# The first RMS norm and the two parts of h at the start of a two-block transformer kernel: squares along rows, multiplied rows turned

## The chip, the core and the metric

The kernel is one program on one core of a Trainium2 chip. Its time is the device time of one execution in microseconds (us). The kernel before takes 2472.72 us, the median of 3 runs (2471.85 to 2472.84).

## The reference, cut to what matters

The reference runs two blocks over one sequence of 512 tokens of width 1024. All numbers are float32. The change concerns the first lines of the first block:

```python
ada = (c @ w_ada[l] + b_ada[l])[:, None, :]
sh1, sc1, gt1, sh2, sc2, gt2 = jnp.split(ada, 6, axis=-1)
h = rms_norm(x, norm1_w[l]) * (1.0 + sc1) + sh1      # x * rsqrt(mean(x*x) + 1e-6) * norm1_w
proj = h @ w_in[l]                                   # 1024 x (4608 + 3360 + 2048)
...                                                  # attention over three dilations, RWKV-7 over 16 heads, gates
x = x + gt1 * ((g_att * y_att + g_rwkv * y_rwkv) @ w_o[l])
...                                                  # conv FFN, then the second block with two layers and their FFNs
```

In the code of the kernel `mod` holds `ada` by columns (partition = feature within a tile of 128, one column for each tile), and `gain1` is `(1 + sc1) * norm1_w`. So tile k of h is `x / rms * gain1[k] + mod[k]`.

## The kernel before

Activations lie with features on the partitions: x and h are 8 tiles (k = 0 to 7) of 128 features by 512 tokens. x arrives by rows (128 tokens on the partitions, 4 groups of 1024 features, tile `x_rows`), and TensorE turns it by multiplying with an identity (`turn`, L312).

Every product of a weight with h is done in three: the weight and h are each split in a high part (rounded to fp32r) and a low part (the rest). TensorE adds w_high x h_high, w_high x h_low and w_low x h_high in a PSUM bank. For a block of weights ("unit", 128 columns) ScalarE makes w_high (`round_unit`, L298) and GpSimd w_low (`lower_unit`, L305). SyncE's queue loads the weights in the order of a ring of four slots; a slot's next load waits for w_low of what was in it.

The order on each engine is written out by hand. The beginning (`begin_pe`, `begin_act`, `begin_dve`) does this:

- SyncE loads x, then 8 blocks of w_ada of 1 MB each (`ada_w`), then four units of w_in. ScalarE's queue loads the first vectors.
- TensorE turns the 32 blocks of x; VectorE and ScalarE copy the 8 turned tiles out of PSUM in turn. ScalarE squares each tile (`sq`), VectorE adds the squares in `rinv`. One product with a matrix of ones sums over the features and spreads the sum to all partitions. VectorE and ScalarE make the root (`rinv`, 128 x 512), and VectorE multiplies the 8 tiles by it into the room of `x_rows` (L548).
- TensorE multiplies c by the blocks of w_ada (`ada_rows_pe`), which gives four lines of 512. VectorE and ScalarE copy two lines each out of PSUM (L447). TensorE makes columns of them (`ada_columns_pe`), VectorE adds the bias and makes `mod` and `gain1` (L453, L458).
- For each tile, ScalarE makes h_high out of the multiplied tile (L525), VectorE makes the shifted tile in float32 (`sq`, L555) and subtracts h_high for h_low (L565). TensorE multiplies the first two units' w_high with both parts as tiles come, and then both w_low with h_high. After that the steady work of the attention stage begins.

`keep_x` stores x to memory for later; it stands in SyncE's queue behind loads of the ring.

Of the kernel before, what the change touches and what calls it, by code (L numbers as in the profile page):

```python
# [15 lines left out]
P = 128  # L16
S = 512
# [103 lines left out]
class Kernel:  # L121
# [327 lines left out]
    def ada_columns_dve(self):  # L449
        V, S_ = self.V, self.S  # L450
        for i in self.ADA_LINES:
# [3 lines left out]
            if i >= 2:  # L455
                at = 4 * (i - 2)
                V.wait_ge(*self.own("dve"))
                V.scalar_tensor_tensor(self.gain1[:, at:at + 4], self.mod[:, 4 * i:4 * i + 4], 1.0,  # L458
                                       self.cols("norm1_w", 4, at), ALU.add, ALU.mult).then_inc(*S_.dve_ada("gain", i))

    def begin_pe(self):
# [7 lines left out]
        for f in range(DT):  # L469
# [5 lines left out]
            self.emptied[b] = (S_.dve_setup if f % 2 else S_.act_setup, ("x", f))  # L475
# [25 lines left out]

    def begin_act(self):
        A, S_ = self.A, self.S
        A.wait_ge(*S_.pool_setup.at("rows"))
        self.load_vectors(0, A, S_.first_loaded)
        for f in range(DT):
            if f % 2 == 0:
                A.wait_ge(*S_.turned.at("x", f))
                A.copy(self.x[:, f, :], self.bank[2 + f % 4][:]).then_inc(*S_.act_setup("x", f))
                A.wait_ge(*self.own("act"))  # L510
            else:
                A.wait_ge(*S_.dve_setup.at("x", f))
            if f >= 2:
                A.wait_ge(*S_.dve_norm.at("norm1", "added", f - 2))
            A.activation(self.sq[:, f % 2, :], self.x[:, f, :], ACT.Square).then_inc(*S_.act_norm("norm1", "square", f))
        A.activation(self.spare[:], self.ones[:, 0:1], ACT.Ln).then_inc(*S_.act_norm())
        self.root_act("norm1")
# [10 lines left out]
    def rooted(self, k):  # L528

        return self.xrow[:].rearrange("p t d -> p (t d)")[:, k * S:(k + 1) * S]  # L530

    def begin_dve(self):
        V, S_ = self.V, self.S
        V.memset(self.rinv[:], 0.0).then_inc(*S_.dve_norm())
        V.wait_ge(*S_.turned.at("vec", 0))
        V.tensor_copy(self.vec[:, 0:P], self.bank[1][:, 0:P]).then_inc(*S_.dve_setup("vec", 0))
        for f in range(DT):
            if f % 2:
# [2271 lines left out]
```

## Time and profile before

| | |
|---|---|
| median of 3 runs | 2472.72 us |
| the profiled execution | 2470.49 us |
| its span, from first to last instruction | 2469.3 us |
| TensorE matmuls busy | 2337.9 us, 95% |
| TensorE weight loads busy | 1847.0 us, 75% |
| VectorE busy | 1433.1 us, 58% |
| ScalarE busy | 686.1 us, 28% |
| GpSimd busy | 882.9 us, 36% |
| mean granted TensorE clock | 0.975 of 2.4 GHz |

The profile is of one execution. Its rows are read as "start, duration, engine, line, operation, output <- inputs, count", and in square brackets the engine's idle time before it and what ended it. A float32 product with a moving operand of 512 columns shows as two records if its weights are float32 and as one if they are fp32r. Records of TensorE overlap their neighbours: what one costs is the distance from start to start. The granted clock is in parts of 2.4 GHz: 0.50 is 1.2 GHz.

### The profile page before, as it was taken

The page shows a single profiled execution, that of the slowest core. Times are in us where ns is not written, and L with a number is a line of the kernel's source. Part 1 is how long each engine was busy: PE and PEld are TensorE (multiplying, and loading weights), DVE is VectorE, ACT ScalarE, POOL GpSimd, SP SyncE. Part 2 cuts the span into 40 slices and gives each one's busy share as a digit, 9 for nine tenths or more (in the row PEclk, how much of TensorE's full clock was granted, in tenths as well). Part 3 has the DMA queues.
Part 4 walks back from the last instruction along what each step waited for, and adds up shares of the span by engine and source line. Part 5 has one row for each costly group of instructions (what it writes and reads, how often), then busy time and mean ns, then how long its engine had stood idle before and what let it go on. Part 6 is the DMA issues. An engine that isn't in the chain of part 4 may idle for free.

```text
span 2469.3 us, 33874 instructions
## 1 busy us (share of the span) xinstructions
PE 2337.9 (95%) x14384; PEld 1847.0 (75%) x14384; DVE 1433.1 (58%) x1805; ACT 686.1 (28%) x854; POOL 882.9 (36%) x415
## 2 busy tenths in 40 slices
PE   6999998999998799899999988999999999999998
PEld 4776775666665688678888866888888887888887
DVE  4221324577667411766675568888863457888733
ACT  3222113434442423222222221322222332322212
POOL 4322221111110344344444433444444444444443
PEclk8999999999999899989999989999999999999999
DMA  6433332212110333223333323233333322333331
GB/s 235 128 103 111 111 103 68 51 41 51 43 45 14 107 98 94 86 77 94 98 112 94 90 62 88 86 102 95 95 110 95 93 86 85 98 98 94 113 94 58
DMA packets 412038, 222.56 MB, mean 90 GB/s; under 512 B 33823, under 2 KB 409458, under 8 KB 410610
## 3 DMA queue, kind: packets, MB, share of 16 engines
q1 hardware_dynamic: 387234, 208.23, 29.2%
q10 hardware_dynamic: 24656, 12.18, 1.8%
q8 instruction: 114, 1.87, 0.3%
q14 instruction: 34, 0.28, 0.0%
HBM read 214.61 MB, written 5.77 MB: 89 GB/s over the span
## 4 chain that ended last, share of the span: by engine, by line
PE 59%; DVE 6%; issue 1%; ACT 1%; POOL 0%; DVEq 0%; ACTq 0%
PE bank L309 59%; DVE ev_s L2406 0%; DVE h_low L2014 0%; DVE mg_r_low L1992 0%; DVE g_c L2216 0%; PE bank L312 0%; DVE ev_low L2418 0%; DVE x_res L2363 0%; DVE sq L653 0%; DVE sq L649 0%; DVE ev_z L2373 0%; DVE ev_c L2375 0%; DVE ev_c L2382 0%; DVE ev_s L2409 0%; DVE sq L2113 0%
## 5 line engine op out<-in xcount | busy, mean ns | idle before, releaser
L305 POOL TENSOR_TENSOR w_low<-w_raw,w_high 128x1024 fp32r<-128x1024 f32 (+1 forms) x331 | 849.5, 2568 | 1494.7 <-ACT w_high L298 1494.6
L309 PE MATMUL bank<-h_high,w_high 128*128 128x512 f32 x2008 | 809.0, 403 | 28.4 <-DVE h_low L660 9.6
L309 PE MATMUL bank<-h_low,w_high 128*128 128x512 f32 x2008 | 789.3, 393 | 0.0
L298 ACT CAST w_high<-w_raw 128x1024 fp32r<-128x1024 f32 (+1 forms) x331 | 358.5, 1084 | 913.2 <-PE bank L309 899.6
L309 PE MATMUL bank<-h_high,w_low 128*128 128x512 f32 x2008 | 510.5, 394 | 0.0
L309 PEld LDWEIGHTS bank<-h_high,w_high 128*128 128x128 f32 x2008 | 379.9, 189 | 133.7 <-issue 24.8
L309 PEld LDWEIGHTS bank<-h_high,w_low 128*128 128x128 f32 x2008 | 377.0, 189 | 84.2 <-issue 4.6
L309 PEld LDWEIGHTS bank<-h_low,w_high 128*128 128x128 f32 x2008 | 381.3, 190 | 78.1 <-issue 3.4
L309 PE MATMUL bank<-g_high,w_high 128*128 128x512 f32 x352 | 138.1, 392 | 2.3 <-ACT g_c L2195 2.3
L309 PE MATMUL bank<-g_low,w_high 128*128 128x512 f32 x352 | 137.8, 391 | 0.0
L2092 DVE TENSOR_TENSOR x_res<-bank,x_res 128x512 f32<-128x512 f32 x32 | 22.1, 692 | 164.8 <-PE bank L309 164.8
L2214 DVE SCALAR_TENSOR_TENSOR g_c<-g_c,vec 128x511 f32<-128x511 f32 x44 | 110.2, 2504 | 1.5
L2225 DVE CAST g_high<-g_c 128x512 fp32r<-128x512 f32 x44 | 102.1, 2320 | 1.5
L2115 DVE TENSOR_TENSOR rinv<-rinv,sq 128x512 f32<-128x512 f32 x48 | 97.5, 2031 | 1.6
L309 PE MATMUL bank<-g_high,w_low 128*128 128x512 f32 x352 | 85.9, 392 | 0.0
L827 DVE COPY att_coming<-bank 128x512 f32<-128x512 f32 x24 | 16.6, 692 | 118.7 <-PE bank L309 118.7
L2240 DVE TENSOR_SCALAR f_c<-bank,vec 128x512 f32<-128x512 f32 x44 | 35.6, 810 | 75.1 <-PE bank L309 72.5
L309 PEld LDWEIGHTS bank<-g_high,w_high 128*128 128x128 f32 x352 | 66.2, 188 | 17.4 <-ACT g_c L2195 3.2
L2195 ACT ACTIVATE g_c<-g_c,vec 128x512 f32<-128x512 f32 x44 | 31.9, 724 | 165.1 <-DVE g_c L2216 165.1
L309 PEld LDWEIGHTS bank<-g_low,w_high 128*128 128x128 f32 x352 | 66.2, 188 | 14.4
L309 PEld LDWEIGHTS bank<-g_high,w_low 128*128 128x128 f32 x352 | 66.2, 188 | 14.4
L1999 DVE TENSOR_TENSOR att_masks<-att_masks,bank 128x512 f32<-128x512 f32 x16 | 10.9, 686 | 109.5 <-PE bank L309 109.5
(375 smaller groups left out, 2886.2 us busy)
## 6 DMA issues: line engine op xcount, KB each, us to landing
w_raw<-in_w_in SPq DMA_DIRECT2D x58, 512.0 KB, 4.7
w_raw<-in_w_up SPq DMA_DIRECT2D x44, 512.0 KB, 3.8
w_raw<-in_w_ffn_gate SPq DMA_DIRECT2D x44, 512.0 KB, 3.8
w_raw<-in_w_ffn_up SPq DMA_DIRECT2D x44, 512.0 KB, 3.8
w_raw<-in_w_ffn_down SPq DMA_DIRECT2D x32, 704.0 KB, 4.5
w_raw<-in_w_ada SPq DMA_DIRECT2D x32, 512.0 KB, 3.6
w_raw<-in_w_down SPq DMA_DIRECT2D x16, 704.0 KB, 4.5
w_raw<-in_w_in ACTq DMA_DIRECT2D x21, 512.0 KB, 4.1
```

The costliest lines, as they stand in the source:

```text
L298: self.A.copy(self.w_high[:, u % SPLIT_SLOTS, 0:k * P], self.raw_of(key)[:, 0:k * P]).then_inc(*self.S.rounded(*key))
L305: self.G.tensor_tensor(self.w_low[:, slot, 0:k * P], self.raw_of(key)[:, 0:k * P], self.w_high[:, slot, 0:k * P].bitcast(F32), ALU.subtrac ...
L309: return self.T.matmul(out, lhsT, rhs, start=start, stop=stop, skip_group_check=True)
L827: return copy(out, in_order(self.bank[b][:], g))
L1999: V.tensor_tensor(self.gate[:, j, :], self.gate[:, j, :], self.bank[4 * (n % 2) + 2 + j][:], ALU.mult).then_inc(*S_.dve_merge())
L2092: V.tensor_tensor(x, bank, x, ALU.add).then_inc(*S_.residual(name, n))
L2115: V.tensor_tensor(total[:], total[:], square, ALU.add).then_inc(*self.S.dve_norm(*key))
L2195: A.activation(gate, gate, ACT.Silu, bias=biases(0)[:, n:n + 1]).then_inc(*S_.silu(name, n))
L2214: V.scalar_tensor_tensor(gate[:, 1:S], scaled[:, 0:S - 1], tap[1], gate[:, 1:S], ALU.mult, ALU.add).then_inc(*S_.parts())
L2225: V.tensor_copy(self.f_high[:, n, :], gate).then_inc(*S_.parts())
L2240: V.tensor_scalar(out, bank[:], tap[2], biases(j)[:, n:n + 1], ALU.mult, ALU.add).then_inc(*S_.parts())
```

## The change

The sum of squares is made along the rows of x as they arrive: ScalarE squares each of the four groups (128 x 1024) and gives the sum of each row (`accum_out`) in `x_root`, 128 x 4. The root is made of these 4 columns. VectorE multiplies the rows in place by it, and copies all 8 turned tiles of x. The multiplied rows are then turned by TensorE a second time (`rooted_pe`), the first before the columns, two more behind them and the others in front of the products of tile k - 3. ScalarE makes h_high directly from PSUM. For even tiles VectorE makes the whole tile (`begin_whole`, from PSUM) and subtracts h_high; for odd tiles ScalarE takes the shift off h_high again (`less`, with `shift_less` = -mod), and VectorE makes h_low with one operation from PSUM. `keep_x` waits for the copies of x.

The diff, without `ada_columns_dve` (it makes `shift_less` behind `mod` for the two shift lines) and the allocations:

```diff
 def begin_pe(self):
...
         for k in range(DT):
-            if k == 3:
-                self.sum_pe("norm1", S_.dve_norm.at("norm1", "squares"))
-                self.emptied[7] = (S_.dve_norm, ("norm1", "mean"))
             self.ada_rows_pe(k)
+        self.emptied[1] = (S_.act_norm, ("row", self.ADA_LINES[-1]))
+        T.wait_ge(*S_.dve_norm.at("norm1", "rooted", 3))
+        self.rooted_pe(0)
         self.ada_columns_pe()
         self.end("pe", "ada")
+        self.rooted_pe(1)
+        self.rooted_pe(2)
...
         for k in range(DT):
+            if k + 3 < DT:
+                self.rooted_pe(k + 3)
             T.wait_ge(*S_.h_low_even.at("norm1", k))
...
+    ROOTED_BANKS = (5, 0, 2, 3, 4, 1, 5, 0)
+    def rooted_pe(self, k):
+        b = self.ROOTED_BANKS[k]
+        self.empty(b)
+        for t in range(4):
+            ins = self.turn(self.bank[b][:, t * P:(t + 1) * P], self.xrow[:, t, k * P:(k + 1) * P])
+        ins.then_inc(*self.S.turned("rooted", k))
+        self.emptied[b] = (self.S.h_low_even, ("norm1", k))
...
 def begin_act(self):
+        for t in range(4):
+            A.wait_ge(*self.own("act"))
+            A.activation(self.sq[:].rearrange("p a t -> p (a t)"), self.xrow[:, t, :], ACT.Square,
+                         accum_out=self.x_root[:, t:t + 1]).then_inc(*S_.act_norm("norm1", "square", t))
         A.activation(self.spare[:], self.ones[:, 0:1], ACT.Ln).then_inc(*S_.act_norm())
-        self.root_act("norm1")
+        A.wait_ge(*S_.dve_norm.at("norm1", "mean"))
+        A.activation(self.x_root[:], self.x_root[:], ACT.Ln).then_inc(*S_.act_norm())
+        A.wait_ge(*self.own("act"))
+        A.activation(self.x_root[:], self.x_root[:], ACT.Exp, bias=0.0, scale=-0.5).then_inc(*S_.act_norm("norm1", "root"))
...
         for k in range(DT):
+            bank = self.bank[self.ROOTED_BANKS[k]]
             A.wait_ge(*S_.dve_ada.at("column", k // 4))
-            A.activation(self.h_high[:, k, :], self.rooted(k), ACT.Identity, bias=self.mod[:, k:k + 1],
+            A.wait_ge(*S_.turned.at("rooted", k))
+            A.activation(self.h_high[:, k, :], bank[:], ACT.Identity, bias=self.mod[:, k:k + 1],
                          scale=self.gain1[:, k:k + 1]).then_inc(*S_.act_norm("norm1", "high", k))
+            if k % 2:
+                if k > 2:
+                    A.wait_ge(*S_.h_low_even.at("norm1", k - 2))
+                A.wait_ge(*S_.dve_ada.at("less", k // 4))
+                A.wait_ge(*self.own("act"))
+                A.activation(self.sq[:, 1, :], self.h_high[:, k, :].bitcast(F32), ACT.Identity,
+                             bias=self.shift_less[:, k:k + 1]).then_inc(*S_.act_norm("norm1", "less", k))
...
 def begin_dve(self):
+        for f in range(DT):
+            V.wait_ge(*S_.turned.at("x", f))
+            V.tensor_copy(self.x[:, f, :], self.bank[2 + f % 4][:]).then_inc(*S_.dve_setup("x", f))
+        V.wait_ge(*S_.act_norm.at("norm1", "square", 3))
+        V.tensor_scalar(self.x_root[:], self.x_root[:], 1.0 / D, RMS_EPS, ALU.mult, ALU.add).then_inc(*S_.dve_norm("norm1", "mean"))
         V.wait_ge(*S_.act_norm.at("norm1", "root"))
-        for k in range(DT):
-            V.tensor_tensor(self.rooted(k), self.x[:, k, :], self.rinv[:], ALU.mult).then_inc(*S_.dve_norm("norm1", "normed", k))
+        for t in range(4):
+            V.tensor_scalar(self.xrow[:, t, :], self.xrow[:, t, :], self.x_root[:, t:t + 1], None,
+                            ALU.mult).then_inc(*S_.dve_norm("norm1", "rooted", t))
...
         self.ada_columns_dve()
+        self.begin_whole(0)
         for k in range(DT):
+            self.begin_low(k)
+            if k % 2 == 0 and k + 2 < DT:
+                self.begin_whole(k + 2)
...
+    def begin_whole(self, k):
+        V, S_ = self.V, self.S
+        V.wait_ge(*S_.act_norm.at("norm1", "high", k))
+        V.wait_ge(*self.own("dve"))
+        V.scalar_tensor_tensor(self.sq[:, 0, :], self.bank[self.ROOTED_BANKS[k]][:], self.gain1[:, k:k + 1],
+                               self.grid(self.mod, k, (0, S)), ALU.mult, ALU.add).then_inc(*S_.dve_norm("norm1", "whole", k))
+    def begin_low(self, k):
+        V, S_ = self.V, self.S
+        if k % 2:
+            V.wait_ge(*S_.act_norm.at("norm1", "less", k))
+            V.scalar_tensor_tensor(self.h_low[:, k, :], self.bank[self.ROOTED_BANKS[k]][:], self.gain1[:, k:k + 1],
+                                   self.sq[:, 1, :], ALU.mult, ALU.subtract).then_inc(*S_.h_low_even("norm1", k))
+        else:
             V.wait_ge(*self.own("dve"))
-            V.scalar_tensor_tensor(self.sq[:, k % 2, :], self.rooted(k), self.gain1[:, k:k + 1],
-                                   self.grid(self.mod, k, (0, S)), ALU.mult, ALU.add).then_inc(*S_.dve_norm("norm1", "shifted", k))
...
+            V.tensor_tensor(self.h_low[:, k, :], self.sq[:, 0, :], self.h_high[:, k, :].bitcast(F32),
+                            ALU.subtract).then_inc(*S_.h_low_even("norm1", k))
```

On VectorE, before, the stretch from the multiplication by the root to the first h_low stands so (`x_rows` is the room of x by rows, L548 the multiplication, L555 the shifted tile):

```order
L548 TENSOR_TENSOR x_rows<-x_res,rinv 128x512 [waits act_norm]
L548 TENSOR_TENSOR x_rows<-x_res,rinv 128x512 x7
L447 COPY ada_line<-bank 1x512 [waits ada_row]
L447 COPY ada_line<-bank 1x512
L453 TENSOR_TENSOR mod<-bank,vec 128x4 [waits ada_row]
L458 SCALAR_TENSOR_TENSOR gain<-mod,vec 128x4 [waits dve_ada]
L453 TENSOR_TENSOR mod<-bank,vec 128x4 [waits ada_row] x2
L458 SCALAR_TENSOR_TENSOR gain<-mod,vec 128x4 [waits dve_ada]
L453 TENSOR_TENSOR mod<-bank,vec 128x4 [waits ada_row]
L555 SCALAR_TENSOR_TENSOR sq<-x_rows,gain,mod 128x512 [waits dve_ada]
L555 SCALAR_TENSOR_TENSOR sq<-x_rows,gain,mod 128x512 [waits dve_norm]
L565 TENSOR_TENSOR h_low<-sq,h_high 128x512 [waits act_norm]
```

In the changed kernel the same stretch of VectorE, from the columns on (line numbers are those of the changed file: L462 is gain, L457 `shift_less`, L586 the whole tile, L597 an even h_low, L593 an odd one):

```order
L453 TENSOR_TENSOR mod<-bank,vec 128x4 [waits ada_row]
L462 SCALAR_TENSOR_TENSOR gain<-mod,vec 128x4 [waits dve_ada]
L453 TENSOR_TENSOR mod<-bank,vec 128x4 [waits ada_row]
L457 TENSOR_SCALAR shift_less<-mod 128x4 [waits dve_ada]
L453 TENSOR_TENSOR mod<-bank,vec 128x4 [waits ada_row]
L462 SCALAR_TENSOR_TENSOR gain<-mod,vec 128x4 [waits dve_ada]
L453 TENSOR_TENSOR mod<-bank,vec 128x4 [waits ada_row]
L457 TENSOR_SCALAR shift_less<-mod 128x4 [waits dve_ada]
L586 SCALAR_TENSOR_TENSOR sq<-bank,gain,mod 128x512 [waits dve_ada,act_norm]
L597 TENSOR_TENSOR h_low<-sq,h_high 128x512 [waits dve_norm]
L586 SCALAR_TENSOR_TENSOR sq<-bank,gain,mod 128x512 [waits h_low_even,act_norm]
L593 SCALAR_TENSOR_TENSOR h_low<-bank,gain,sq 128x512 [waits act_norm]
```

The multiplication by the root has left the place in front of the columns' work, two small operations have come between the `mod`s, and odd tiles have one large operation instead of two.

On TensorE, the difference around the first products of h (L312 is a turn; `bank<-ident,x_rows` the second turning; - is before, + the changed kernel):

```order
+L312 MATMUL bank<-ident,x_rows 128x128 [waits dve_ada]
+L312 MATMUL bank<-ident,x_rows 128x128 x3
 L309 MATMUL bank<-h_high,w_high 128x512 [waits rounded,h_low_even]
 L309 MATMUL bank<-h_low,w_high 128x512
-L309 MATMUL bank<-h_high,w_high 128x512 [waits dve_norm,rounded]
-L309 MATMUL bank<-h_low,w_high 128x512
+L309 MATMUL bank<-h_high,w_high 128x512 [waits rounded]
+L309 MATMUL bank<-h_low,w_high 128x512
+L312 MATMUL bank<-ident,x_rows 128x128 [waits dve_ada]
+L312 MATMUL bank<-ident,x_rows 128x128 x3
 L309 MATMUL bank<-h_high,w_high 128x512 [waits h_low_even]
```

Four turns now stand ahead of the products of each of the first tiles, and a product's place in the queue is behind them.

## Rows read from the trace of the kernel before

**Rows 1.** Table by stretch: us, each engine's busy time, clock, DMA.

```profile
core 0: us, PE busy (x) PEld busy (x) DVE busy (x) ACT busy (x) POOL busy (x), PEclk, DMA share, GB/s
...
20.00:24.00 4.00, 0.00 (x0) 0.00 (x0) 2.68 (x4) 2.59 (x5) 0.00 (x0) 0.96 1.02 426
...
31.00:34.00 3.00, 0.02 (x4) 0.00 (x0) 3.00 (x6) 2.41 (x4) 0.57 (x1) 0.99 1.19 295
34.00:42.10 8.10, 4.50 (x32) 4.42 (x33) 6.18 (x13) 3.91 (x6) 6.84 (x7) 0.50 0.31 77
42.10:47.40 5.30, 5.30 (x13) 4.01 (x14) 5.19 (x8) 2.66 (x4) 2.30 (x5) 0.50 0.77 198
47.40:52.70 5.30, 5.12 (x21) 3.70 (x20) 3.92 (x6) 0.00 (x0) 0.00 (x0) 0.98 0.01 2
```

**Rows 2.** TensorE in order of time: start, duration, instruction, idle before.

```profile
26.05 4.97 PE L309 MATMUL bank<-ada_w,vec 128*1 128x512 f32 x40
35.16 4.50 PE L309 MATMUL bank<-ones,ada_line 1*128 1x1 f32 x32 [4.14 <-DVE ada_line L447]
42.10 0.79 PE L309 MATMUL bank<-h_high,w_high 128*128 128x512 f32 x1 [2.43 <-DVE h_low L565]
...
52.71 3.80 PE L309 MATMUL bank<-h_high,w_low 128*128 128x512 f32 x16
```

**Rows 3.** TensorE's weight loads, around the last block of w_ada.

```profile
26.05 0.11 PEld L309 LDWEIGHTS bank<-ada_w,vec 128*1 128x1 f32 x8 [1.50 <-issue]
26.86 0.15 PEld L309 LDWEIGHTS bank<-ada_w,vec 128*1 128x1 f32 x4 [0.71 <-issue]
...
29.56 0.10 PEld L309 LDWEIGHTS bank<-ada_w,vec 128*1 128x1 f32 x4 [0.33 <-DMA ada_w<-in_w_ada]
```

**Rows 4.** VectorE in order of time, the same stretch.

```profile
29.48 4.91 DVE L548 TENSOR_TENSOR x_rows<-x_res,rinv 128x512 f32<-128x512 f32 x8 [2.64 <-ACT rinv L620]
34.42 1.42 DVE L447 COPY ada_line<-bank 1x512 f32<-1x512 f32 x2
37.06 0.16 DVE L453 TENSOR_TENSOR mod<-bank,vec 128x4 f32<-128x4 f32 x1 [1.23 <-PE bank L309]
37.26 1.65 DVE L458 SCALAR_TENSOR_TENSOR gain<-mod,vec 128x4 f32<-128x4 f32 x1
...
39.90 1.54 DVE L555 SCALAR_TENSOR_TENSOR sq<-x_rows,gain,mod 128x512 f32<-128x512 f32 x2
41.36 0.69 DVE L565 TENSOR_TENSOR h_low<-sq,h_high 128x512 fp32r<-128x512 f32 x1
...
50.02 1.41 DVE L565 TENSOR_TENSOR h_low<-sq,h_high 128x512 fp32r<-128x512 f32 x2
```

**Rows 5.** ScalarE in order of time.

```profile
31.10 1.18 ACT L447 COPY ada_line<-bank 1x512 f32<-1x512 f32 x2 [1.65 <-PE bank L309]
...
33.78 1.04 ACT L298 CAST w_high<-w_raw 128x1024 fp32r<-128x1024 f32 x1 [0.44 <-DMA w_raw<-in_w_in]
39.02 5.74 ACT L525 ACTIVATE h_high<-x_rows,mod,gain 128x512 fp32r<-128x512 f32 x8 [4.19 <-DVE mod L453]
```

**Rows 6.** GpSimd in order of time.

```profile
33.43 5.46 POOL L305 TENSOR_TENSOR w_low<-w_raw,w_high 128x1024 fp32r<-128x1024 f32 x2 [15.52 <-ACT w_high L298]
```

**Rows 7.** Groups of ScalarE's instructions, whole run, by shape: busy, mean ns.

```profile
L1267 ACT ACTIVATE x_res<-bank,vec 128x512 f32<-128x512 f32 x8 | 5.5, 688 | 35.0 <-PE bank L309 35.0
...
L1073 ACT ACTIVATE rw_low_g<-rw_low_g 128x1024 f32<-128x1024 f32 x1 | 1.1, 1062 | 0.0
```

**Rows 8.** One VectorE line: min/median/max ns.

```profile
L653 DVE TENSOR_SCALAR sq<-sq,mod x8: 486/486/1376, 1045.5 to 1059.2; 128x512 f32<-128x512 f32 x8
```

**Rows 9.** TensorE, the turns of x.

```profile
9.56 4.70 PE L312 MATMUL bank<-ident,x_rows 128*128 128x128 f32 x24
```

**Rows 10.** The same turns, 9.5 to 11.5: mean ns.

```profile
L312 PE MATMUL bank<-ident,x_rows 128*128 128x128 f32 x10 | 2.3, 421 | 0.0
```

**Rows 11.** The same turns, 13.5 to 14.4.

```profile
L312 PE MATMUL bank<-ident,x_rows 128*128 128x128 f32 x7 | 1.1, 299 | 0.0
```

More of the change, by code:

```diff
@@ L454, in ada_columns_dve @@
                             ALU.add).then_inc(*S_.dve_ada("column", i))
-            if i >= 2:
+            if i < 2:
+                V.wait_ge(*self.own("dve"))
+                V.tensor_scalar(self.shift_less[:, 4 * i:4 * i + 4], self.mod[:, 4 * i:4 * i + 4], -1.0, None,
+                                ALU.mult).then_inc(*S_.dve_ada("less", i))
+            else:
                 at = 4 * (i - 2)
@@ L505, in begin_act @@
         self.load_vectors(0, A, S_.first_loaded)
[L506 to L515, printed above, removed]
+        self.meet("act", "setup", ("pool",))
+        A.activation(self.spare[:], self.ones[:, 0:1], ACT.Square).then_inc(*S_.act_norm())
+        A.wait_ge(*S_.x_loaded.at("x"))
+        for t in range(4):
+            A.wait_ge(*self.own("act"))
+            A.activation(self.sq[:].rearrange("p a t -> p (a t)"), self.xrow[:, t, :], ACT.Square,
+                         accum_out=self.x_root[:, t:t + 1]).then_inc(*S_.act_norm("norm1", "square", t))
         A.activation(self.spare[:], self.ones[:, 0:1], ACT.Ln).then_inc(*S_.act_norm())
-        self.root_act("norm1")
+        A.wait_ge(*S_.dve_norm.at("norm1", "mean"))
+        A.activation(self.x_root[:], self.x_root[:], ACT.Ln).then_inc(*S_.act_norm())
+        A.wait_ge(*self.own("act"))
+        A.activation(self.x_root[:], self.x_root[:], ACT.Exp, bias=0.0, scale=-0.5).then_inc(*S_.act_norm("norm1", "root"))
         A.wait_ge(*S_.ada_row.at("rows"))
@@ L537, in begin_dve @@
         for f in range(DT):
-            if f % 2:
-                V.wait_ge(*S_.turned.at("x", f))
-                V.tensor_copy(self.x[:, f, :], self.bank[2 + f % 4][:]).then_inc(*S_.dve_setup("x", f))
-            V.wait_ge(*S_.act_norm.at("norm1", "square", f))
-            V.wait_ge(*self.own("dve"))
-            V.tensor_tensor(self.rinv[:], self.rinv[:], self.sq[:, f % 2, :], ALU.add).then_inc(*S_.dve_norm("norm1", "added", f))
-        S_.dve_norm.table["norm1", "squares"] = S_.dve_norm.value
-        self.sum_dve("norm1")
+            V.wait_ge(*S_.turned.at("x", f))
+            V.tensor_copy(self.x[:, f, :], self.bank[2 + f % 4][:]).then_inc(*S_.dve_setup("x", f))
+        V.wait_ge(*S_.act_norm.at("norm1", "square", 3))
+        V.tensor_scalar(self.x_root[:], self.x_root[:], 1.0 / D, RMS_EPS, ALU.mult, ALU.add).then_inc(*S_.dve_norm("norm1", "mean"))
         V.wait_ge(*S_.act_norm.at("norm1", "root"))
-        for k in range(DT):
-            V.tensor_tensor(self.rooted(k), self.x[:, k, :], self.rinv[:], ALU.mult).then_inc(*S_.dve_norm("norm1", "normed", k))
+        for t in range(4):
+            V.tensor_scalar(self.xrow[:, t, :], self.xrow[:, t, :], self.x_root[:, t:t + 1], None,
+                            ALU.mult).then_inc(*S_.dve_norm("norm1", "rooted", t))
         V.wait_ge(*S_.ada_row.at("rows"))
@@ L2691, in keep_x @@
     def keep_x(self):
-        self.Y.wait_ge(*self.S.dve_norm.at("norm1", "normed", DT - 1))
+        self.Y.wait_ge(*self.S.dve_setup.at("x", DT - 1))
         self.Y.dma_start(self.io["kept"], self.x[:].rearrange("p k t -> p (k t)")).then_inc(*self.S.x_kept("x"))
@@ L2710, in build @@
         self.rinv_first, self.gain_even = self.sb("rinv_first", [P, S]), self.sb("gain_even", [P, DT])
+        self.x_root, self.shift_less = self.sb("x_root", [P, 4]), self.sb("shift_less", [P, DT])
         self.gain1, self.gain2 = self.sb("gain1", [P, DT]), self.sb("gain2", [P, DT])
```

17 lines of the change are left out of this document (4 added, 13 removed).

## The prediction

> **What bounds the kernel now.** The page's first part shows TensorE busy for 95% of the span, and its fourth part gives 59% of the ending chain to TensorE's one matmul line. A change in the beginning can therefore pay only while TensorE is not yet the bound. I read the table by stretch first [rows 1]: TensorE does nothing from 20 to 24 us and from 31 to 34, and little matmul work until 42.1. The granted clock falls with the idleness (0.50 from 34 to 47.4, that is 1.2 GHz) and is back at 2.4 GHz after it. Then I read each engine in order of time [rows 2 to 6]. The blocks of w_ada set the first part: the weight load at 29.56 still ends its wait by a DMA [rows 3], and the products on it end at 26.05 + 4.97 = 31.02 [rows 2]. From there the chain is: VectorE still multiplies x by the root until 34.39, so it copies its two ada lines from 34.42; TensorE's columns start at 35.16; the first `mod` is made at 37.06; its gain takes 1.65 us instead of a fraction, until 38.91, beside GpSimd's two w_low, which end at 33.43 + 5.46 = 38.89 [rows 4, 6]; h_low of tile 0 ends at 42.05 and TensorE's products of h begin at 42.10 [rows 2, 4]. The 32 products of high weights last until 52.71, the first five microseconds at 0.50, the rest paced by VectorE, whose last h_low ends at 51.43 [rows 1, 2, 4]. At 52.71 TensorE is the bound, and I take every later instruction to move with this one. So the question is: when do the w_low products start, now 52.71?
>
> **Until 31.0: nothing gained or lost but cover.** The change removes 8 squares of 512, 8 sums, the ones-matmul, mean, and two 512-wide roots. It adds 4 squares over 1024 with a row sum. No row has a square with a sum; the nearest 1024-wide activation is 1.06 us [rows 7], so 4.2 us from x's arrival at 9.5 [rows 9], or at most about double, 8.5 us, until 18. Beside the squares VectorE makes 8 copies of x from PSUM, 0.7 each (the ada line copies take 1.42 / 2 [rows 4]), from about 10.7, when the first tile is turned, until 16.3. Mean, logarithm, a table load and exponential are about 2 us more: 18.4. The four row multiplications read SBUF: a 512-wide one takes 0.49 us [rows 8], so 1024 cost between 0.9 and 0.98, together 3.9 us. Everything is ready at 18.4 + 3.9 = 22.3 us, at the upper bound near 26, and the w_ada blocks hold until 31.02. 5 us of cover remain, so these edits are priced at nothing. The ones-matmul leaves TensorE's queue, so each w_ada block is multiplied as it lands; the last still lands at 29.56. The danger is the clock: the eight records from 26.05 to 26.86, behind the idle stretch, took 0.81 us, and all forty took 4.97, 0.99 for eight including those that were slow; at 1.2 GHz a block of eight is 1.6 to 1.7 us instead of 0.85 [rows 2, 3]. If short bursts leave it at 1.2 GHz, the end comes 0.85 us later. I take zero.
>
> **31.0 to the first product of h.** Removed from VectorE's path: the wait for the last row multiplication, 34.42 - 31.1 = 3.3 us. Turn 0 (four turns, 0.4 to 0.66 us) lies under VectorE's first line copy, 1.42 / 2 = 0.71 us. The columns start near 31.85. The first `mod` came 1.9 us after their start at the lower clock [rows 2, 4]; the clock is still 0.99 until 34 [rows 1], so between 0.95 and 1.9: 32.8 to 33.75. Now the catch. ScalarE's order until w_high is unchanged, so GpSimd's w_low still run 33.43 to about 38.2 (two took 38.89 - 34.39 = 4.5 us once VectorE's last row multiplication, at 34.39, was out of the way; the w_high of both are ready by 34.82 [rows 5], so 33.43 + 4.5 to 4.8). What VectorE has to do there grew from two small SBUF-only operations to four: gain, less, gain, less. The row of gain says such an operation waits out a w_low. I take that all four get through only by 38.2 to 38.5. Then `whole` 0 (0.75) and h_low 0 (0.69), with ScalarE's h_high 0 long done, end at 40.4. First product 40.45: 1.65 us earlier than 42.10. Bounds: without that wait, VectorE follows TensorE's columns (4.50 us long, ended 36.4 at the latest), and the first product is at 38.1, 4.0 us earlier; with the slow last block, 0.85 later.
>
> The Trainium skill, page "SBUF — State Buffer", section "Who interferes with whom", says that a VectorE instruction with two SBUF inputs, or a tensor_scalar in the two-port mode, shares ports with GpSimd and that the one that comes second is blocked for the whole instruction. The trace agrees for gain (1.65 us, end 38.91 against w_low's 38.89). By that rule `less` waits too, and the sum stays as it is; it also makes `whole` and the odd h_low, which read PSUM now, free of GpSimd, where no run of before shows it for them.
>
> **The pass over h, from 40.45 on.** Before, a tile k cost VectorE a shifted tile and an h_low, about 1.45 us (8 from 39.90 to 51.43), ScalarE 5.74 / 8 = 0.72 us [rows 5], TensorE four products: 0.42 each at 0.50 (13 records in 5.3 us [rows 1]), 0.23 at 2.4 GHz (16 in 3.80 [rows 2]). Now a pair of tiles costs VectorE `whole` 0.75 + h_low 0.69 + odd h_low 0.75 = 2.2 us, less than 2.9. ScalarE pays two h_high from PSUM at 0.69 [rows 7] and a `less` at about 0.72 to 0.8: 2.2 us. But they now wait for each other: the odd `less` waits for h_low two tiles before, since both use one scratch tile, and stands in ScalarE's queue ahead of the next h_high; `whole` of the next even tile waits for that h_high, and stands ahead of the odd h_low. The circle is less, h_high, whole, h_low: 0.75 + 0.69 + 0.75 + 0.75 = 2.95 us with 0.05 per handover, 3.1 us a pair, 1.57 a tile. That is a little more than the 1.45 of before. TensorE, too, gets work that it did not have: turns 4 to 7 stand between the products (turns 1 to 3 are done before 40.45). Four turns take 10 records in 2 us near 10 us, 0.15 to 0.2 each, and 7 in 0.9 later, 0.13 [rows 10, 11]: 0.5 to 0.8 us for each k.
>
> Step by step at 1.2 GHz: products 0 until 42.15, turn 4 until 42.9, products 1 until 44.6, turn 5 until 45.3; then the clock rises, 5 us after the products' start, as it was in before (42.10 to about 47.4 [rows 1]). At 2.4 GHz: products 2 until 46.3, turn 6 until 46.8, products 3 until 47.7, turn 7 until 48.2. ScalarE gets h_high 7 out at about 49.0, then `less` 7 at 50.3, and VectorE h_low 7 at 51.1 to 51.4. The last four products end at 52.0 to 52.4. I take 52.3, against 52.71: 0.4 us earlier. So 1.65 us of head start shrink to 0.4, since the circle takes 10.8 to 11 us from h_low 0 to h_low 7 where before it was 51.43 - 42.05 = 9.4.
>
> **Moved elsewhere.** SP's store of x for later waits now for the copies of x (16 us) instead of the multiplied rows; in SP's queue it stands behind loads that wait for w_low of the first units, so it doesn't start sooner. POOL's order is the same.
>
> **Sum.** Against the profiled run's 2470.49 us (span 2469.3 and 1.2 around it): 0 until 31.0, -1.65 to the first product, +1.25 in the pass, 0 behind: -0.4, 2470.1. The median of the runs is 2.2 us above that profiled run; so -0.4 on 2472.72 gives 2472.3.
>
> **Rivals.**
> A, the forecast: a change of -0.4 us; with its handovers uncertain, -1.7 to +0.9. Chance 0.5.
> B, small operations aren't held up. For it: mod and `whole` read PSUM, and the ada columns at 2.4 GHz bring the first gain at 33.2, before w_low starts at 33.43. Against it: gain 3 (the second of the two) and `less` come later in any case. First product at 38.1; the pass lasts about 11.4 us at VectorE's and ScalarE's pace, with TensorE's last four products 0.95 behind: 50.1 or so, a change of -2.6. Should the circle also run at the 1.1 us a tile of the engines' own work, -4: 2468.7. Chance 0.2.
> C, slower: the clock. TensorE's work in the pass at 1.2 GHz is 32 x 0.42 + 4 x 0.7 = 16.2 us. Every microsecond longer at that level costs half a microsecond as long as TensorE is the one waited for; from a rise later than about 46.2 the change is slower than before. If it stays until the pass ends, 40.45 + 16.2 = 56.7, or +4.0; with the slow last w_ada block (0.85) +4.8: 2477.5. For it: after 31 us TensorE has only columns and turns, and beside the columns of before the clock read 0.50 throughout (4.50 busy of 8.1 us [rows 1]). Against: the clock of before was back 5.3 us after the products began, and these begin and follow each other much like those. The lower half of this case, +0.9 to +2.5, is the likelier one. Chance 0.2.
> D, the change is absorbed: a later stage (a store, a weight load) ends at its own time; then zero whatever the beginning does. Against: at 52.71 TensorE goes on without a wait [rows 2]. Chance 0.1.
>
> **How the numbers follow.** A measurement of this kernel tells 0.2%, 4.9 us, from no change. A and D lie inside wholly; of B only its end at -4 with luck passes -4.9 (0.04 in all); of C only with the slow block and the low-weight pass slow as well (0.04). So within 0.2%: 0.92. Range: A's own is 2471.0 to 2473.6; to hold 8 in 10 it takes most of B (to -3.2: 2469.5) and the likelier half of C (+2.2: 2474.9).
>
> **What would show it.** In the changed profile: `x_rows` multiplications over by 26 us and no VectorE work between them and the ada lines; ada lines from 31.1 on both engines; gain or less of 1 to 2.5 us beside w_low; first product of h near 40.5 (B: near 38); h_high and `less` alternately waiting for h_low in the pass; clock back at about 45.5 (C: after 47); w_low products from 52.3. If ada rows end at 31.9, the price of short bursts was wrong. If squares plus roots end later than 31, the cover was.

## The result, and the profile after

The changed kernel takes 2482.15 us (median of 6 runs, 2479.25 to 2485.19), the kernel before beside it 2472.78 (6 runs, 2469.14 to 2473.69): 9.4 us slower, ratio 1.0046 with a 95% interval of 1.0035 to 1.0056. The forecast was 2472.3, range 2469.5 to 2474.9. The profiled execution took 2485.19 us (span 2484.0) against 2470.49 before; it is the slowest of its six, so the two spans differ by more than the 9.4 us. Every median here leaves out one execution of two_tiles_alone that took 4665 us, where its ten others took 2475.5 to 2482.1.

The beginning went partly as forecast. By stretch (us, each engine's busy time, granted clock, DMA), against [rows 1]:

```profile
core 0: us, PE busy (x) PEld busy (x) DVE busy (x) ACT busy (x) POOL busy (x), PEclk, DMA share, GB/s
20.00:24.00 4.00, 1.36 (x12) 0.10 (x8) 1.14 (x2) 0.00 (x0) 0.00 (x0) 0.94 1.01 420
24.00:31.00 7.00, 5.02 (x24) 0.32 (x24) 0.00 (x0) 0.00 (x0) 0.00 (x0) 0.50 1.06 374
31.00:34.00 3.00, 3.00 (x18) 2.10 (x14) 1.39 (x2) 2.25 (x4) 0.00 (x0) 0.50 1.20 290
34.00:42.10 8.10, 6.93 (x42) 6.13 (x41) 7.18 (x12) 4.51 (x6) 7.28 (x11) 0.59 0.36 88
42.10:47.40 5.30, 5.30 (x31) 4.29 (x30) 3.77 (x6) 3.73 (x6) 0.66 (x1) 1.00 0.77 200
```

TensorE in order of time (start, duration, instruction, idle before), against [rows 2]:

```profile
29.75 1.89 PE L309 MATMUL bank<-ada_w,vec 128*1 128x512 f32 x8 [0.82 <-DMA ada_w<-in_w_ada]
31.57 1.11 PE L312 MATMUL bank<-ident,x_rows 128*128 128x128 f32 x4
32.61 4.50 PE L309 MATMUL bank<-ones,ada_line 1*128 1x1 f32 x32
37.05 2.90 PE L312 MATMUL bank<-ident,x_rows 128*128 128x128 f32 x12
41.12 0.50 PE L309 MATMUL bank<-h_high,w_high 128*128 128x512 f32 x1 [1.17 <-DVE h_low L597]
...
51.25 3.11 PE L309 MATMUL bank<-h_high,w_low 128*128 128x512 f32 x13
```

The clock fell earlier than before: it is 0.50, 1.2 GHz, from 24 us on, and the last block of w_ada takes 1.89 us and ends at 31.6 (before 31.02). It also came back earlier: from 42.1 on it is 1.00, 2.4 GHz, where [rows 1] has 0.50. Just before that TensorE had done turns 1 to 3 (37.05 to 39.95), where before it stood idle for 2.43 us [rows 2]. The w_low products start at 51.25 instead of 52.71: in this pair of profiles the beginning is 1.46 us shorter. That alone proves little: in the seven profiles with the old beginning untouched (before and experiments 1, 3, 4, 5, 6 and 12) they start anywhere from 51.38 to 52.94.

VectorE, against [rows 4], and GpSimd, against [rows 6]:

```profile
18.39 2.74 DVE L568 TENSOR_SCALAR x_rows<-x_rows,x_root 128x1024 f32<-128x1024 f32 x4 [1.79 <-ACT x_root L537]
31.70 1.42 DVE L447 COPY ada_line<-bank 1x512 f32<-1x512 f32 x2 [10.57 <-PE bank L309]
34.51 0.16 DVE L453 TENSOR_TENSOR mod<-bank,vec 128x4 f32<-128x4 f32 x1 [1.39 <-PE bank L309]
34.71 1.69 DVE L462 SCALAR_TENSOR_TENSOR gain<-mod,vec 128x4 f32<-128x4 f32 x1
...
36.50 2.22 DVE L457 TENSOR_SCALAR shift_less<-mod 128x4 f32<-128x4 f32 x1
...
38.81 0.16 DVE L462 SCALAR_TENSOR_TENSOR gain<-mod,vec 128x4 f32<-128x4 f32 x1
...
39.49 0.75 DVE L586 SCALAR_TENSOR_TENSOR sq<-bank,gain,mod 128x512 f32<-128x512 f32 x1
40.28 0.79 DVE L597 TENSOR_TENSOR h_low<-sq,h_high 128x512 fp32r<-128x512 f32 x1
...
42.62 0.69 DVE L597 TENSOR_TENSOR h_low<-sq,h_high 128x512 fp32r<-128x512 f32 x1
...
45.49 0.69 DVE L597 TENSOR_TENSOR h_low<-sq,h_high 128x512 fp32r<-128x512 f32 x1
```
```profile
34.03 4.66 POOL L305 TENSOR_TENSOR w_low<-w_raw,w_high 128x1024 fp32r<-128x1024 f32 x2 [16.54 <-ACT w_high L298]
```

Gain and shift_less each wait out a w_low (1.69 and 2.22 us, where the next gain takes 0.16); the pass then goes at 2.87 us a pair (42.62 to 45.49).

So the loss lies behind the point where the prediction let everything move along. The last of the three FFN-like stages shows it best: eight residual additions, one behind each 66 products of a down projection (line L2124 is L2092 of before). First and last start, before, then after:

```profile
L2092 DVE TENSOR_TENSOR x_res<-bank,x_res x8: 691/692/692, 2350.8 to 2456.5; 128x512 f32<-128x512 f32 x8
```
```profile
L2124 DVE TENSOR_TENSOR x_res<-bank,x_res x8: 692/692/693, 2362.0 to 2469.3; 128x512 f32<-128x512 f32 x8
```

Between them lie 7 x 66 = 462 products: 105.7 us before, 107.3 after, 228.8 and 232.3 ns from product to product. TensorE waits for nothing here and the clock is full; the same products go slower. What differs for them is where their operands lie: `x_root` (16 bytes in a partition) and `shift_less` (32) stand ahead of `gain1`; each counts as 32 bytes in the order of allocation, so every later tile moves up by 64 bytes.

### The profile page after: what moved, and what is told of

Same layout as the page of the kernel before. It is cut to its first block, busy times and chain, and to the rows that moved or that the text cites. A ratio compares the mean times of both kernels' runs of the same rounds, so it can differ in the third digit from the quotient of the medians.

```text
span 2484.0 us, 33926 instructions
## 1 busy us (share of the span) xinstructions
PE 2353.2 (95%) x14414; PEld 1852.5 (75%) x14414; DVE 1424.1 (57%) x1794; ACT 686.6 (28%) x855; POOL 881.1 (35%) x415
## 4 chain that ended last, share of the span: by engine, by line
PE 60%; DVE 5%; ACT 0%; issue 0%; POOL 0%; DVEq 0%; ACTq 0%
PE bank L309 60%; DVE ev_s L2438 0%; DVE mg_r_low L2024 0%; DVE h_low L2046 0%; DVE g_c L2248 0%; DVE x_res L2395 0%; DVE sq L685 0%; PE bank L312 0%; DVE sq L681 0%; DVE ev_low L2450 0%; DVE ev_z L2405 0%; DVE sq L2145 0%; DVE ev_c L2407 0%; DVE ev_c L2414 0%; DVE ev_s L2436 0%
## 5 line engine op out<-in xcount | busy, mean ns | idle before, releaser
L2124 DVE TENSOR_TENSOR x_res<-bank,x_res 128x512 f32<-128x512 f32 x32 | 22.1, 692 | 174.4 <-PE bank L309 174.4
```

Source lines behind the costliest of these rows:

```text
L2124: V.tensor_tensor(x, bank, x, ALU.add).then_inc(*S_.residual(name, n))
```

## The experiments

Each was timed in five rounds against the kernel before on the same chip (2472.5, 2472.4, 2471.1 and 2472.2 us in the four groups: 1 to 4, 5 to 8, 9 and 10, 11 and 12). Ratios stand with their 95% intervals. Rates are ns from product to product in the profiled execution, the mean over a stage's 128x512 products; addresses are worked out from the order of allocation in slots of 32 bytes, not read from a trace, and rows of the moving operands are 2048 bytes apart, so one remainder modulo 256 holds for a whole tile.

```
kernel                     merge a / r: address, ns     FFN stages: address, ns   w_low at  w_low->merge   whole run
before                     128      227.3 / 226.7       192      228.9            52.71     796.9          -
after                      192      230.2 / 228.9         0      232.4 - 233.3    51.25     800.5          +9.4
1 two_tiles_alone          192      230.3 / 228.9         0      232.4 - 233.4    51.50     794.2          +6.8
2 change_unshifted         128      227.3 / 226.7       192      228.9            50.52     802.9          +1.6
3 shift_128                  0      232.5 / 233.3        64      233.3 - 233.5    51.97     795.1          +7.4
4 shift_192                 64      233.3 / 233.3       128      226.7 - 227.3    52.86     798.9          -3.6
5 late_64                  128      226.9 / 226.7         0      232.4 - 233.3    52.94     796.2          +7.9
6 late_192                 128      226.7 / 226.7       128      226.7 - 227.0    51.38     797.4          -3.1
7 low_waits                128      226.8 / 226.7       192      228.9            50.46     801.5          +1.6
8 low_waits_late_192       128      227.1 / 226.7       128      226.7 - 227.1    52.04     802.1          -2.0
9 31_turns                 128      227.3 / 226.7       192      228.9            53.39     801.8          +4.6
10 change_64_turns         128      226.8 / 226.7       192      228.9 - 229.3    53.33     799.4          +2.1
11 change_freed            128      227.0 / 226.7       128      226.7 - 227.4    53.95     793.9          -3.6
12 late_192_again          128      226.7 / 226.7       128      226.7 - 227.1    52.55     799.2          -3.7
```

(w_low at: start of the first w_low product of the beginning, us; w_low->merge: us from there to the first product of the merge; whole run: median less the median of before. Only the last column is of many runs, 5 to 12 of them; all others are of one profile each.)

**1, two_tiles_alone.** The kernel before with the two tiles allocated where the change has them, and unused.

```diff
         self.rinv_first, self.gain_even = self.sb("rinv_first", [P, S]), self.sb("gain_even", [P, DT])
+        self.x_root, self.shift_less = self.sb("x_root", [P, 4]), self.sb("shift_less", [P, DT])
```

> The kernel before, with nothing but the two new tiles of the change (x_root and shift_less) allocated at their place and never used. All tiles behind them in SBUF start 64 bytes per partition later. Theory P (place): the 1968 products of the FFN, even and odd stages whose moving operand starts at 124096 + 64 take 232.4 ns from start to start instead of 229, which is 6.7 us, and the RWKV and merge stages lose about 3 more: 2482 to 2484 us, with the beginning as in before (w_low products at 52.7). Theory B (the code of the beginning does it, through its clock or its order on later stages): 2472.8, within 1 us.

2479.38 us (10 runs), ratio 1.0027 [1.0017, 1.0037]. Two tiles that nothing reads or writes cost 6.8 us, by the interval 4.2 to 9.1; that is less than the 9 to 11 expected.

**2, change_unshifted.** The whole change, with the two tiles in the beginning's own scope behind `vec_rows`, where nothing of before moves.

> The changed kernel with x_root and shift_less allocated behind vec_rows, in the scope of the beginning, so that no tile of before moves. Theory P: the beginning's own gain alone is left, 1.5 us (51.25 against 52.71 in the traces): 2471.3 us, between 2470 and 2472.5; g_high products at 229 ns. Theory B: as the changed kernel, 2481 to 2483.

2474.09 us, 1.0006 [0.9996, 1.0016], which is not told from no change. By the medians experiments 1 and 2 add up to 6.8 + 1.6 = 8.4 us, against 9.4 measured (8.7 to 13.8 by its interval). The last down projection, rate as before:

```profile
L2124 DVE TENSOR_TENSOR x_res<-bank,x_res x8: 690/691/692, 2356.4 to 2462.1; 128x512 f32<-128x512 f32 x8
```

**3 and 4, shift_128 and shift_192.** The kernel before with 128 or 192 unused bytes ahead of `gain1` (`[P, 32]`, `[P, 48]`).

```diff
+        self.pad = self.sb("pad", [P, 32])
         self.gain1, self.gain2 = self.sb("gain1", [P, DT]), self.sb("gain2", [P, DT])
```

> The kernel before with an unused tile of 128 bytes per partition ahead of gain1. P, in the form that the place modulo 256 bytes counts (128 gives 227 ns, 192 gives 229, 0 gives 232.4 in the two traces): the FFN tiles are at 64, where no trace has a price; by the distance from 128 it is 229 as before, and the merge and RWKV tiles, at 0, lose 5 to 7 us: 2478. If the place modulo 128 counts, FFN tiles are at 64 and all others at 0 as in before: 2472.8. B: 2472.8 too, but with no product changed in its rate.

> The kernel before with an unused tile of 192 bytes per partition ahead of gain1. P modulo 256: FFN, even and odd tiles at 128, where h_high is, so 227 ns instead of 229: -4.1 us; merge and RWKV tiles at 64: +0.6 and +2.5. Sum 2471 to 2472. P modulo 128: FFN tiles at 0 and the others at 64, FFN -4, the others as after the 64 byte shift, +3: also 2472, so the rates by tile tell: mg products 229, f and g products 227. B: 2472.8 and no rate changed.

2479.94 us, 1.0030 [1.0018, 1.0042], and 2468.94, 0.9989 [0.9980, 0.9997]. With 192 bytes the FFN stages land at remainder 128 and run at 226.7; the merge lands at 64 and runs at 233.3, but has 288 products against 1968. So it isn't the size of the shift but where it puts the moving operand. The products on h_high and h_low are the control: these tiles lie ahead of every pad, and their median from product to product is 227 ns in all fourteen profiles.

**5 and 6, late_64 and late_192.** The pad behind the shared tiles, so only the FFN stages move.

```diff
         shared.close()
+        self.pad = self.sb("pad", [P, 16])
```

> The kernel before with an unused tile of 64 bytes per partition allocated only behind the merge stage, so that FFN, even and odd stage tiles stand where the changed kernel has them and RWKV and merge tiles where before has them. P: 1968 products at 232.4 instead of 229 ns, +6.7 us: 2479.5. B: 2472.8.

> The kernel before with an unused tile of 192 bytes per partition allocated only behind the merge stage: the FFN, even and odd tiles start at 124288, 128 modulo 256 as h_high does; RWKV and merge stay. P: 1968 products at 227 instead of 229 ns, -4.1 us: 2468.7. B: 2472.8.

2480.29 us, 1.0034 [1.0024, 1.0044], and 2469.23, 0.9989 [0.9981, 0.9998]. The last down projection in late_64 and in late_192:

```profile
L2092 DVE TENSOR_TENSOR x_res<-bank,x_res x8: 692/693/693, 2360.3 to 2468.1; 128x512 f32<-128x512 f32 x8
```
```profile
L2092 DVE TENSOR_TENSOR x_res<-bank,x_res x8: 691/692/692, 2348.4 to 2453.1; 128x512 f32<-128x512 f32 x8
```

107.8 and 104.7 us for the same 462 products. It shows in the groups of the whole run too, by the mean ns of one product (before, after, late_192):

```profile
L309 PE MATMUL bank<-g_high,w_low 128*128 128x512 f32 x352 | 85.9, 392 | 0.0
```
```profile
L309 PE MATMUL bank<-g_high,w_low 128*128 128x512 f32 x352 | 87.0, 395 | 0.0
```
```profile
L309 PE MATMUL bank<-g_high,w_low 128*128 128x512 f32 x352 | 85.0, 389 | 0.0
```

The 64-byte cost sits in the FFN stages: late_64 costs no less than the two early tiles do. 1968 products by 3.5 to 4.4 ns are 6.9 to 8.7 us; measured 7.9.

**7, low_waits.** change_unshifted, with GpSimd's first w_low held back until the last `shift_less`, to see what the wait for w_low costs.

```diff
+        self.G.wait_ge(*self.S.dve_ada.at("less", 1))
```

> The changed kernel unshifted (as e2), and GpSimd's first two w_low wait until VectorE has made the last shift_less. Port theory: gain and less take 0.16 to 0.2 us each instead of 1.7 and 2.2, whole 0 starts at about 37.2 instead of 39.5, the first product of h at about 38.8 instead of 41.1; the w_low products then start near 49 to 50 instead of 51.25, w_low being ready long before. 1 to 2 us less than e2: 2469.8. Rival, TensorE's columns and turns set the place: the first product stays near 40 to 41 and the time is that of e2.

2474.00 us, 1.0015 [1.0004, 1.0027]: nothing gained. Its VectorE and GpSimd:

```profile
34.48 0.16 DVE L462 SCALAR_TENSOR_TENSOR gain<-mod,vec 128x4 f32<-128x4 f32 x1
...
35.36 0.17 DVE L457 TENSOR_SCALAR shift_less<-mod 128x4 f32<-128x4 f32 x1
...
37.42 0.75 DVE L586 SCALAR_TENSOR_TENSOR sq<-bank,gain,mod 128x512 f32<-128x512 f32 x1
38.21 2.08 DVE L597 TENSOR_TENSOR h_low<-sq,h_high 128x512 fp32r<-128x512 f32 x1
```
```profile
37.38 5.15 POOL L305 TENSOR_TENSOR w_low<-w_raw,w_high 128x1024 fp32r<-128x1024 f32 x2 [19.90 <-DVE shift_less L457]
```

Gain and shift_less now take 0.16 and 0.17. But h_low 0, from two tiles in SBUF, ran beside the w_low instead and took 2.08 where it took 0.78 in change_unshifted; `whole` 0, which reads PSUM, took its usual 0.75 beside the same w_low. So the first product starts at 40.34, against 40.41 in change_unshifted. The wait moved with the w_low, and in both orders something on the path met it.

**8, low_waits_late_192.** Both together.

> The kernel of e7 with the 192 byte tile of e6. The parts should add: -4.1 for the place of the late tiles, -1.5 for the change itself, -1.5 for the wait: 2466 us. If they don't add, the difference shows what is shared between them.

2470.33 us, 0.9987 [0.9977, 0.9998]: the medians of 6 and 7 add up to -1.5, measured -2.0, and the 2466 expected had counted gains that 7 didn't bring. Its beginning is that of low_waits, and TensorE's turns 1 to 3 run from 36.56 to 39.38, where in low_waits they run from 36.82 to 39.64. Yet the clock came back only at 44.8, and in low_waits at 39.9, so that the pass over h took 11.97 us instead of 10.12:

```profile
34.00:42.10 8.10, 7.40 (x38) 6.50 (x38) 6.08 (x13) 4.63 (x7) 4.99 (x2) 0.50 0.27 67
42.10:47.40 5.30, 5.30 (x26) 4.38 (x25) 2.80 (x4) 2.90 (x5) 3.12 (x10) 0.74 0.78 204
```

**9, 31_turns.** What was left: change_unshifted starts its w_low products 2.2 us earlier in its profile (50.52) and still ends later. From there to the merge it takes 802.9 us, low_waits and low_waits_late_192 801.5 and 802.1, after 800.5, and before and the five other kernels measured so far with the old beginning 794.2 to 798.9. TensorE pauses in it for nothing that the profile shows, before `rw_keep` products and turns, and its program is 31 instructions longer. So: the kernel before, with 31 idle turns of the identity into an unused bank.

```diff
             self.ada_rows_pe(k)
+            for t in range(4 if k < DT - 1 else 3):
+                self.turn(self.bank[6][:, t % 4 * P:(t % 4 + 1) * P], self.ident[:])
```

> The kernel before with 31 more turns of the identity on TensorE, into a bank that nobody uses yet: four behind each of the first seven blocks of w_ada, three behind the last. TensorE's program then holds 12178 instructions, as many as the changed kernel's, against 12147; VectorE, ScalarE, GpSimd and all tiles are as in the kernel before. Theory P (where TensorE's instructions stand in its queue makes the pauses that no wait explains): between 684 and 817 us the same pause of about 1.2 us appears in front of a product on rw_keep near 732, a pause of about 1.5 in front of the turn near 681, and the stretch from the first w_low product to the first merge product is longer than before's 796.9 us by 4 to 6 (801 to 803); about 2477 us if the beginning itself costs nothing. Rival Q (what costs 4 to 5 us later hangs on what the new beginning did on the other engines): no pauses, 794 to 799 us as in the six kernels with the old beginning, 2472 to 2473 us in all.

2475.69 us, 1.0017 [1.0008, 1.0026], and 801.8 us to the merge. TensorE's waits put down to "issue" (us in total, times, longest) from 575 to 735 us: before; change_unshifted (beside it a turn at 680.58 that waited 1.79 us, put down to VectorE); and 31_turns:

```profile
PE bank L312 <- issue: 0.6, 1, 0.6
```
```profile
680.58 0.66 PE L312 MATMUL bank<-ident,rw_k 128*128 128x128 f32 x4 [1.79 <-DVE rw_ends L1463]
...
PE bank L309 <- issue: 1.2, 1, 1.2
```
```profile
PE bank L309 <- issue: 3.0, 2, 1.8
```

With the old beginning and only 31 more instructions in TensorE's queue two such pauses appear at the same places, 3.0 us. The whole run takes 4.6 us more (2.0 to 6.4 by the interval), and the stretch 4.9 more than in the profile of before, 2.6 to 7.6 more than in the seven with the old beginning untouched. All seven profiles with more instructions have two pauses of 1.2 to 1.8 us: near 681 and 731 us with 31 more (after and experiments 2, 7, 8 and 9), near 582 and 632 with 64 more (10 and 11). Of the seven without, six have none over 0.7 us, but two_tiles_alone has one, in front of a turn at 727.72:

```profile
PE bank L312 <- issue: 1.5, 1, 1.5
```

So in 31_turns more instructions ahead cost time, and the pauses go with the place in the queue; that nothing else makes one is not shown. Part of the 4.6 us may lie in the beginning, since the w_low products start at 53.39, 0.45 us behind the latest of the seven untouched. Nor do the pauses account for the stretch: they are 2.4 us of the 4.9, the rest has no cause here, and change_freed, with two pauses, has the shortest stretch of all (793.9). Why they come is only made likely: the trace has a DMA queue of kind "instruction" that brings 16 KB at a time (114 packets, 1.87 MB), and in after and in experiments 2, 9, 10 and 11 the last product ahead of each of the ten pauses starts 0.5 to 1.0 us after such a packet starts, and the pause ends 1.2 to 1.5 us after it has landed. For the longest one in 31_turns (last product 681.62, next 683.61; the packet 681.0 to 682.1), the queues between 680.5 and 683.5:

```profile
q10 hardware_dynamic: 571, 0.28, 32.6%
q1 hardware_dynamic: 576, 0.03, 13.1%
q8 instruction: 1, 0.02, 2.2%
```

In these stages TensorE runs 64x64 products, up to 61 in a microsecond (before, 678 to 679), and a packet comes each 4 to 19 us, where in the FFN stages it is about each 28. Such packets come in the kernel before too, but there no pause put down to "issue" is over 0.6 us in this stretch.

**10, change_64_turns.** change_unshifted with 33 more such turns, 64 later in all.

> The changed kernel with its two tiles where they move nothing (as change_unshifted), with 33 more turns of the identity behind its blocks of w_ada (four behind seven of them, five behind the last): TensorE's instructions behind the beginning then stand 64 places later than in the kernel before, where in change_unshifted they stand 31 later. Theory P with places that count in powers of two up to 64: the pauses at 681 and 732 us go and the stretch from the first w_low product to the first merge product is again 795 to 799 us instead of 802.9; about 2470 us. Theory P without such a period: the pauses move to other places, time anywhere from 2470 to 2477. Rival Q: pauses and 801 to 803 us as in change_unshifted, 2474 us.

2473.25 us, 1.0005 [0.9996, 1.0014]; to the merge 799.4, just outside the first case. The two pauses are gone from 681 and 731, and two like them end at 585.57 and 635.2 (1.30 us, in front of a product on `rw_keep`).

```profile
585.57 0.66 PE L312 MATMUL bank<-ident,rw_b 128*128 128x128 f32 x4 [1.65 <-issue]
```

So a shift by 64 doesn't restore the old state, but moves the pauses, as the second case had it. Here the clock came back at 45.9 and the w_low products start at 53.33.

**11 and 12, change_freed and late_192_again.** change_unshifted with 33 turns ahead of all other TensorE work and the 192-byte pad of late_192; beside it late_192 once more.

> The changed kernel's beginning without both of its side effects: its two tiles move nothing (as change_unshifted), 33 turns of the identity stand ahead of all other work of TensorE, while it waits for the first loads, so that its later instructions stand 64 places behind those of the kernel before (as change_64_turns), and the tiles behind the merge lie 192 bytes later (as late_192). If place in memory and place in the queue are all that cost time, the w_low products start at 50.5 to 52 us as in the other kernels with this beginning, the stretch from them to the merge is 795 to 800 us, and the whole is 2467 to 2469 us, equal to or up to 2 us below late_192_again on the same chip. If the new beginning costs something later by itself (the granted clock that falls near 143 us in every kernel that has it), it is 1.5 to 3 us above late_192_again.

> The kernel before with 192 unused bytes behind the shared tiles, once more, beside change_freed: 2469 us, 3 to 4 us below before as it was, under either reading.

2468.61 us, 0.9988 [0.9979, 0.9996], and 2468.43, 0.9988 [0.9979, 0.9997]. Equal, and both beat before and after: with its tiles well placed the new beginning gains nothing that the runs can tell, nor does experiment 2 show a gain. change_freed isn't free of the second effect, since it has two pauses (1.2 us each, to 581.55 and 631.03). To the merge change_freed takes 793.9 us, but its pass over h fell into the case that the prediction called C:

```profile
34.00:42.10 8.10, 5.12 (x42) 4.07 (x42) 7.15 (x11) 4.98 (x7) 6.84 (x9) 0.70 0.32 88
42.10:47.40 5.30, 5.30 (x18) 4.24 (x18) 3.59 (x6) 1.64 (x3) 1.08 (x3) 0.50 0.76 198
```

Clock 0.50 from 42.1 to 47.4, 18 matmuls where after has 31, and w_low products from 53.95. A granted clock of 0.76 around 142 to 149 us, which I had put to the new beginning, is also in late_192_again with the old one, and not in change_freed. It is in five of the six profiles with the new beginning and in one of the eight with the old, so it isn't bound to the change, but whether the change makes it likelier is open. 7 us at 0.76 lose about 1.7, an estimate.

## Why the prediction was wrong

**The step that failed** is "At 52.71 TensorE is the bound, and I take every later instruction to move with this one", and the term "0 behind" in the sum. That TensorE is the bound was right, and it is just why this failed: the same products can take longer on TensorE without a wait or a slower clock. In place of "0 behind" the runs have +6.8 us for the place of the tiles (experiment 1; 5 and 6 put it in the FFN stages) and +4.6 us for 31 more instructions in TensorE's queue (experiment 9). Less a beginning 1.5 us shorter in the profile that makes 9.9; measured 9.4, closer than the terms themselves are known. The first part is shown, also in the rate of the products. The second is known only to about 2 us either way, and what makes it is open; experiment 2, the change with the tiles in place, costs 1.6 us in all. The diff had the line that allocates the two tiles, and the prediction gave it no term. The rivals held nothing like it: all of them ended at 52.71. Rival C gave the right sign in its number, 2477.5, for a reason that did not occur in this kernel's profile.

**Until 31.0.** The squares took 4.7 us from 9.28, between the two estimates (4.2 and 8.5) and near the lower: four of 1.06 us, each with 0.19 for reading out the sum,

```profile
12.83 1.06 ACT L531 ACTIVATE sq<-x_rows 128x1024 f32<-128x1024 f32 x1
13.79 0.19 ACT L531 ACTIVATION_READ_ACCUMULATOR sq<-x_rows 128x1 f32 x1
```

done at 14.0. The row multiplications took 0.69 each, not 0.9 to 0.98, and ended at 21.1 (forecast 22.3). They were done 8.6 us ahead of the last block's products (29.75), so the cover held. The danger named there came true: the last block took 1.89 us at 1.2 GHz, 0.6 us later than before, which the prediction priced at 0.85 and took as zero.

**To the first product of h.** Forecast 40.45, measured 41.12; 0.6 us of the difference come from that late block (31.64 instead of 31.02), behind which ScalarE's w_high and GpSimd's w_low start 0.6 later too (34.03 instead of 33.43). The catch was right in kind and size: gain 1.69, shift_less 2.22, the last gain at 38.81, h_low 0 over at 41.07. The Trainium skill's rule ("SBUF — State Buffer", "Who interferes with whom") is that a VectorE instruction with two SBUF inputs, or a tensor_scalar in a two-port mode, contends with GpSimd, and one with at most one SBUF input outside these modes doesn't. The trace agrees: gain and h_low (two inputs, 1.69, and 2.08 in experiment 7) and `shift_less` (a tensor_scalar, 2.22) wait, `whole` (PSUM, 0.75 in experiment 7) doesn't. Rival B, 38.1, was wrong for this reason, and in experiment 7, without the wait on the small operations, the first product still starts at 40.34. (Its own terms, 38.1 + 11.4 + 0.95, add up to 50.45 and not to 50.1.)

**The pass.** Forecast 11.85 us (40.45 to 52.3), measured 10.13 (41.12 to 51.25). The circle of less, h_high, whole and h_low was right, 2.87 us a pair against 2.95 to 3.1. Mis-sized was the clock: it rose at about 40.6, ahead of the first product, and not at 45.3; so turns and products cost half. That turns alone can bring it up is seen at the start of this kernel and of before: TensorE has done only turns when, at about 13.3 us, the clock reaches 2.4 GHz and their records go from 0.42 to 0.27 us (also [rows 10, 11]). So turns 1 to 3 are the likely cause here too, but when it rises isn't fixed by them: in experiment 8 the same turns had run, it rose at 44.8, and the pass took 11.97 us (40.08 to 52.04), as forecast. Of the four profiles of this beginning without added turns three have a pass of 10.1 us and one of 12.0, so the gain of 1.46 us is in part luck of the execution. In experiment 11, at 0.50 until 47.4, it took 12.28 us (41.67 to 53.95). Rival C is real, worth 2.2 us against after's pass and not 4. The old pass doesn't hang on it: it took 10.58 to 10.62 us in all eight profiles with the old beginning, with the clock back anywhere from 45.0 to 48.2.

**Absorption (D)** isn't tested by itself: from w_low to merge the profiles of the old beginning already differ by 5 us (794.2 to 799.2), more than what the beginning could gain.

## What to carry to other kernels

Where TensorE is the bound, look at everything in a diff that moves addresses or the length of its queue, even an allocation of a few bytes or instructions in a stage long over; to test a change by itself, put new small tiles behind all others or into a scope that is closed. Then compare the same stage's product-to-product time in both traces before looking for a wait. A saving of 1.5 us at one end of a kernel is less than either side effect here (6.8 and 4.6 us), and less than what single profiles of one beginning differ by; so the version to keep was the old kernel with 192 unused bytes: 3.1 and 3.7 us faster in two groups of runs.

## What was not expected of the hardware

- The rate of 128x512 fp32r products depends on the start of the moving operand in SBUF: 226.7 to 227.4 ns with remainder 128 modulo 256 bytes, 228.9 with 192, 232.4 to 233.3 with 0, 233.3 with 64 (stages of 528 to 1056 products; the merge's smaller stages give 226.7 to 233.3 in the same order, with up to 232.5 at 0 and 230.3 at 192 in one of them). Whether the stationary operand or other engines' access has a part in it was not tried.
- TensorE pauses of 1.2 to 1.8 us that no wait explains come with more instructions ahead in its queue (two in each of seven profiles, one in one of the seven others); they follow packets of the instruction queue in stages of many small products.
- With the short instructions out of the way of GpSimd's w_low, the next two-input instruction takes the wait (gain 0.16 for 1.70, h_low 2.08 for 0.78).
- The same beginning can find the clock back at 39.9 or at 44.8 us (experiments 7 and 8), and its pass over h then takes 10.12 or 11.97 us.
